# A Trainium2 decoder kernel's S5 stage: the output matrix made in compact form by VectorE and spread into blocks by ScalarE

## The reference, cut to what matters

```python
ab_re, ab_im, bb_re, bb_im = s5_discretize(lam_re, lam_im, log_dt, b_re, b_im)
bu_re = jnp.einsum("btgc,gpc->btgp", u, bb_re)
...
_, _, s_re, s_im = lax.associative_scan(_s5_combine, (a_re, a_im, bu_re, bu_im), axis=1)
y = (jnp.einsum("btgp,gcp->btgc", s_re, c_re.astype(jnp.float32))
     - jnp.einsum("btgp,gcp->btgc", s_im, c_im.astype(jnp.float32)))
```

## Time and profile before

| what | value |
|---|---|
| median of 3 runs | 3703.88 us (3703.57 to 3706.3) |
| the profiled execution, its own time | 3705.97 us |
| its span in the profile | 3704.4 us |
| TensorE matmul busy | 2222.4 us (60%) |
| VectorE busy | 2701.0 us (73%) |
| ScalarE busy | 590.1 us (16%) |
| GpSimd busy | 1227.0 us (33%) |
| S5 stage (to the first GLU product) | the first 232.5 us |

### The profile page before, as it was taken

How to read it: one execution, slowest core, us unless ns; L and a number is a source line. 1 busy time by engine, 2 the same in 40 slices (tenths; PEclk the granted TensorE clock), 3 DMA queues, 4 the chain that set the end, 5 groups by cost and what they waited for, 6 DMA issues and landing times.

```text
span 3704.4 us, 30645 instructions
## 1 busy us (share of the span) xinstructions
PE 2222.4 (60%) x9874; PEld 1420.6 (38%) x9874; DVE 2701.0 (73%) x3594; ACT 590.1 (16%) x1349; POOL 1227.0 (33%) x1366
## 2 busy tenths in 40 slices
PE   5789960002777786594997676440598771004776
PEld 5777750001222276593662366430254220001222
DVE  9931399998875588977578667869758559997554
ACT  6621100000111122200111112100111110000111
POOL 2110133433344332223333422224433444334332
PEclk9999985556999997797999988775799995557999
DMA  4023489999999999999999999999999999999998
GB/s 125 24 98 125 152 359 391 424 427 427 426 416 427 427 425 426 416 426 427 427 421 387 427 425 426 426 426 427 427 426 407 425 427 427 427 427 427 427 427 357
DMA packets 201715, 1407.16 MB, mean 380 GB/s; under 512 B 21856, under 2 KB 30304, under 8 KB 30768
## 3 DMA queue, kind: packets, MB, share of 16 engines
q0 software_dynamic: 167008, 1215.18, 78.1%
q1 hardware_dynamic: 34288, 190.10, 12.9%
q10 hardware_dynamic: 288, 0.18, 0.0%
HBM read 1402.13 MB, written 3.24 MB: 379 GB/s over the span
## 4 chain that ended last, share of the span: by engine, by line
DMA 40%; DVE 27%; PE 23%; issue 5%; ACT 4%; POOL 0%; DVEq 0%; POOLq 0%; ACTq 0%
DMA arena<-in_u_dram,ixs 27%; PE ps L937 15%; DVE arena L1782 14%; DMA arena<-in_v_dram,ixs 13%; PE ps L623 3%; ACT arena L1313 2%; DVE ps L1798 2%; PE ps L835 2%; PE ps L666 1%; DVE arena L1673 1%; DVE arena L1666 1%; DVE arena L1557 1%; DVE arena L1667 1%; DVE arena L1670 1%; DVE arena L1663 1%
## 5 line engine op out<-in xcount | busy, mean ns | idle before, releaser
L937 PE MATMUL ps<-arena 128*128 128x512 f32 x2304 | 1119.2, 616 | 1145.0 <-ACT arena L1313 1093.3
L1782 DVE CUSTOM_DVE_ANT_0 arena<-arena,ps 128x2048 f32<-128x2048 f32 x546 | 1234.1, 2286 | 195.7 <-DMA arena<-in_u_dram,ixs 177.3
L1798 DVE SCALAR_TENSOR_TENSOR ps<-arena,ps 128x1024 f32<-128x1024 f32 x564 | 727.0, 1289 | 532.2 <-DMA arena<-in_v_dram,ixs 513.0
L937 PEld LDWEIGHTS ps<-arena 128*128 128x128 f32 x2304 | 405.5, 192 | 1831.0 <-issue 953.3
L510 POOL DMA_INDIRECT arena<-in_u_dram,ixs x560 | 553.2, 988 | 1091.1 <-DVE arena L1782 1026.8
L510 POOL DMA_INDIRECT arena<-in_v_dram,ixs x576 | 558.7, 970 | 935.5 <-PE ps L937 634.2
L835 PE MATMUL ps<-HT,W 128*128 128x160 f32 (+1 forms) x3072 | 406.8, 294 | 73.5 <-ACT arena L1263 30.7
L835 PEld LDWEIGHTS ps<-HT,W 128*128 128x128 f32 x3072 | 401.3, 197 | 93.2 <-issue 76.8
L1313 ACT ACTIVATE arena<-ident,arena 128x128 f32<-128x128 f32 x576 | 228.4, 400 | 1005.7 <-PE ps L937 973.9
L863 PE MATMUL ps<-W,arena 128*128 128x128 f32 x1024 | 124.9, 283 | 41.2 <-DVE arena L1904 14.9
L863 PEld LDWEIGHTS ps<-W,arena 128*128 128x128 f32 x1024 | 121.1, 198 | 43.7 <-DVE arena L1904 15.1
(11 more groups left out here) (291 smaller groups left out, 1764.5 us busy)
## 6 DMA issues: line engine op xcount, KB each, us to landing
W<-in_slabs_dram SPq DMA_DIRECT2D x168, 1024.0 KB, 9.9
arena<-in_u_dram,ixs POOLq DMA_INDIRECT x576, 16.5
arena<-in_v_dram,ixs POOLq DMA_INDIRECT x576, 16.7
HN<-in_s_bc_dram SPq DMA_DIRECT2D x16, 256.0 KB, 3.3
GB<-in_norms_dram POOLq DMA_DIRECT2D x4, 1024.0 KB, 12.1
X<-in_x_dram SPq DMA_DIRECT2D x3, 1024.0 KB, 13.7
W<-in_x_dram SPq DMA_DIRECT2D x8, 256.0 KB
out_y_dram<-HN SPq DMA_DIRECT2D x2, 1024.0 KB, 6.8
```

Of the source, the lines that this page charges most:

```text
L937: mm = nc.tensor.matmul(ps[:, 8 - SHARE + b, :], DG[(first + n) % DIAGS], ring[:, r, OWN + BANK * b:OWN + BANK * (b + 1)], start=(n == 0), ...
L1782: V.tensor_tensor_reduce(ring[:, r, :], ring[:, r, :], token, 1.0, 0.0, ALU.mult, ALU.add, AV[:, COL_AT[t] + n:COL_AT[t] + n + 1]).then_in ...
L1798: V.scalar_tensor_tensor(to, row, weight, total, ALU.mult, ALU.add).then_inc(row_used[r], 1)
```

## The change

`output_matrices(n)` no longer writes the four blocks of `OMX`. VectorE waits (`s5_ca`) until ScalarE has read the last compact matrix, and subtracts at full width, 128x512, twice, into two new buffers `CS`. ScalarE has a new step `output_blocks(n)`, between `chunk_columns(n+1)` and `kernels(n)`: it waits for `s5_cs` and `s5_y`, copies `CS` into the blocks of `OMX` by four copies of 64x512, and raises `s5_ca`, which so far VectorE raised. `input_matrices` keeps its four half-width subtractions, written out in place. `CS` lies in space that nothing else uses during the stage. No transfer is added or moved.

```diff
--- before.py
+++ after.py
@@ -228,6 +228,7 @@
         SP = [view(2 * D + 2 * PQ * CHUNKS * h, 2 * PQ * CHUNKS, w_flat).rearrange("p (c q j) -> p c q j", c=2, q=PQ)
               for h in range(2)]
         DEC = [view(2 * D + 4 * PQ * CHUNKS + 512 * h, 512, w_flat).rearrange("p (q j) -> p q j", q=PQ) for h in range(2)]
+        CS = [view(16384, 512), view(7424, 512, w_flat)]
         S0 = GB[:, 1, 0:1024].rearrange("p (c q b) -> p c q b", c=2, q=S5_Q)
         SSO = GB[:, 1, 1024:2048].rearrange("p (c q b) -> p c q b", c=2, q=S5_Q)
         U4 = ht_flat.rearrange("p (q j) -> p q j", q=S5_Q)
@@ -313,7 +314,7 @@
         s5_bc_in = [sem("s5_bc_in0"), sem("s5_bc_in1")]
         s5_bcc, s5_dd, s5_h, s5_ends = sem("s5_bcc"), sem("s5_dd"), sem("s5_h"), sem("s5_ends")
         s5_ph, s5_f, s5_tab, s5_dec = sem("s5_ph"), sem("s5_f"), sem("s5_tab"), sem("s5_dec")
-        s5_ab, s5_ca, s5_pad = sem("s5_ab"), sem("s5_ca"), sem("s5_pad")
+        s5_ab, s5_cs, s5_ca, s5_pad = sem("s5_ab"), sem("s5_cs"), sem("s5_ca"), sem("s5_pad")
         s5_k, s5_kc = sem("s5_k"), sem("s5_kc")
         s5_bs, s5_c0, s5_g = sem("s5_bs"), sem("s5_c0"), sem("s5_g")
         s5_tp, s5_tc = sem("s5_tp"), sem("s5_tc")
@@ -1097,6 +1098,18 @@
                             scale=(1.0, -1.0)[c])
                 ins.then_inc(s5_c0, 1)
 
+            def output_blocks(n):
+
+                act.wait_ge(s5_cs, n + 1)
+                if n > 0:
+                    act.wait_ge(s5_y, n)
+                for c in range(2):
+                    for h in range(2):
+                        rows = slice(64 * h, 64 * (h + 1))
+                        ins = A(OMX[rows, c, :, 1:, 16 * h:16 * (h + 1)], CS[c][rows].rearrange("p (q s n) -> p q s n", q=PQ, s=LC),
+                                ACT.Copy)
+                ins.then_inc(s5_ca, 1)
+
             def kernels(n):
 
                 act.wait_ge(s5_k, n + 1)
@@ -1150,6 +1163,7 @@
                 if more:
                     turned_inputs(n + 1)
                     chunk_columns(n + 1)
+                output_blocks(n)
                 kernels(n)
                 if n > 0:
                     token_rows(n - 1)
@@ -1540,7 +1554,7 @@
                 V.scalar_tensor_tensor(PRD, plus, ROUND, PRD, ALU.subtract, ALU.subtract).then_inc(s5_f, 1)
                 dve.wait_ge(s5_f, n + 1)
 
-            def scaled(to, n, first, tables, free):
+            def scaled(n, first, tables):
 
                 qs, cube4 = slice(PQ * n, PQ * (n + 1)), [P, PQ, LC, 16]
                 re, im, neg = (w[:, :, qs].rearrange("p s q -> p q s").unsqueeze(3).to_broadcast(cube4) for w in tables)
@@ -1550,34 +1564,33 @@
                 V.tensor_tensor(t[1], b, im, ALU.mult)
                 V.tensor_tensor(t[2], a, neg, ALU.mult)
                 settle(V.tensor_tensor(t[3], b, re, ALU.mult))
-                free()
+                return t
+
+            def input_matrices(n):
+
+                dve.wait_ge(s5_bcc, n + 1)
+                t = scaled(n, 0, (GFR, GFI, GFN))
+                if n > 0:
+                    dve.wait_ge(s5_tp, S5_TURN[INPUT, n - 1, 3] + 1)
+                    dve.wait_ge(s5_bs, n)
                 for c in range(2):
                     for h in range(2):
                         rows = slice(64 * h, 64 * (h + 1))
-                        ins = V.tensor_tensor(to[rows, c, :, :, 16 * h:16 * (h + 1)], t[2 * c][rows], t[2 * c + 1][rows],
+                        ins = V.tensor_tensor(IMX[rows, c, :, :, 16 * h:16 * (h + 1)], t[2 * c][rows], t[2 * c + 1][rows],
                                               ALU.subtract)
-                return ins
-
-            def input_matrices(n):
-
-                def free():
-                    if n > 0:
-                        dve.wait_ge(s5_tp, S5_TURN[INPUT, n - 1, 3] + 1)
-                        dve.wait_ge(s5_bs, n)
+                ins.then_inc(s5_ab, 1)
+                dve.wait_ge(s5_ab, n + 1)
+
+            def output_matrices(n):
 
                 dve.wait_ge(s5_bcc, n + 1)
-                scaled(IMX, n, 0, (GFR, GFI, GFN), free).then_inc(s5_ab, 1)
-                dve.wait_ge(s5_ab, n + 1)
-
-            def output_matrices(n):
-
-                def free():
-                    if n > 0:
-                        dve.wait_ge(s5_y, n)
-
-                dve.wait_ge(s5_bcc, n + 1)
-                scaled(OMX[:, :, :, 1:], n, 2, (PWR, PWI, PWN), free).then_inc(s5_ca, 1)
-                dve.wait_ge(s5_ca, n + 1)
+                scaled(n, 2, (PWR, PWI, PWN))
+                if n > 0:
+                    dve.wait_ge(s5_ca, n)
+                for c in range(2):
+                    ins = V.tensor_tensor(CS[c], T[2 * c], T[2 * c + 1], ALU.subtract)
+                ins.then_inc(s5_cs, 1)
+                dve.wait_ge(s5_cs, n + 1)
 
             def states(n):
```

## The result

The changed kernel takes **3731.13 us** (median of 6 runs, 3727.30 to 3732.37), the kernel before in the same session 3704.08 (3703.55 to 3708.13): a ratio of 1.0068, 95% interval [1.0057, 1.0080], or +27 us. Slower, as forecast; but the forecast was 3716.7, and the range ended at 3729.0. The rival that came true is the first one, with the clock much worse (3722 to 3733).

A forecast was written before the change was run, and what follows sets the result against it. The loop through ScalarE's compaction and TensorE's kernel was taken as the bound, not VectorE's occupancy. Place-by-place terms of +7.4 us plus +5.4 for the clock gave +12.8 on 3703.88: 3716.7 us, range 3706.5 to 3729.

The forecast's parts named there:

- the first one, with the clock much worse: Rival: transposes and kernels at the low clock in most pairs, +18 to +29 us, 3722 to 3733; chance 0.17.
- the clock's price for the transposes: TensorE's input transposes, slower behind a longer pause: 0.4 us a pair, over six pairs.
- The bound: S5 loop of compaction, matrices, TensorE's kernel, ScalarE's copies, 23.68 us; VectorE, nearly full, waits once a pair for the compaction.
- The copies and the route: Four ScalarE copies ahead of the kernel take 2.49 us; ScalarE's route becomes 13.11 us against 11.76, +1.35 a pair.
- kernel term: TensorE's kernel product, slower by the clock behind a longer pause: 0.5 us a pair.
- the predicted loop: One middle pair of the S5 stage by the route alone: 25.03 us for 23.68.
- the mechanism and the bound: Sixteen transposes wholly at the low clock take 2.2 us more; ScalarE's copies hide all but 1.4.
- outputs 0 and kernel 7: TensorE restarts used to size the clock term: 2.46 us idle then 5.13 low; 3.15 idle then 5.46, no more than now.
- The pause itself: TensorE's pause behind the outputs, ahead of the input transposes: to grow from 1.29 to 2.3 us.
- The outputs' wait for the states: TensorE's outputs no longer wait 0.96 us for the states, so the pause behind them grows.
- GpSimd's collision: GpSimd's phases may hold up an input matrix instead of the output matrix; ScalarE's route hides it, otherwise 0.7 us a pair.
- the sum of +12.8: Whole forecast loss: +7.4 us from the places in the S5 stage and +5.4 from the clock.

The follow-up runs named there:

- e4: Changed kernel with its two full-width subtractions cut into four of 64 rows each; 3728.46 us, ratio 1.0062.
- e1: Changed kernel plus 16 extra TensorE transposes of a constant ahead of each pair's input transposes and 16 ahead of its kernel product; 3703.01 us, ratio 0.9993.
- e10: Changed kernel plus 16 extra TensorE transposes ahead of each pair's input transposes alone; 3721.23 us, ratio 1.0041.
- e15: Changed kernel with GpSimd's phase held back until VectorE's input subtractions are done; 3728.26 us, ratio 1.0063.
- e12: Changed kernel with the second half of each pair's outputs held back on TensorE until VectorE's third product of the next input matrix; 3719.78 us, ratio 1.0041.
- e6: Changed kernel with ScalarE's compaction of the next input moved ahead of its kernels copy; 3709.03 us, ratio 1.0012.
- e3: Kernel before plus the change's four ScalarE copies at the same queue place, into spare buffers nobody waits for; 3704.67 us, ratio 0.9996.
- e14: e6 with TensorE's kernel product begun on the output matrix's real part, the imaginary part afterwards, all sums complete; 3698.23 us, ratio 0.9980.

## Why the prediction was wrong

The term that failed is the clock's price for the transposes, 0.4 us a pair: the stretch that holds them grew by 1.87.

- **The bound, right.** The loop led through the compaction, not through VectorE's 22.9 busy microseconds. e4 undoes VectorE's gain at no cost that can be measured.
- **The copies and the route, right.** Four copies of 2.52 us (2.49 predicted). From the last chunk copy to the next kernel's copies +1.80 us, where route and kernel term, 1.35 + 0.5, gave 1.85; the kernel took 5.98 us for some 5.4 before. With the clock held up, e1 has 23.73 us a pair; the predicted loop of 25.03, with e1's kernel of 3.88 us in place of 5.4, is 23.5.
- **Where it failed: "0.4 for the transposes".** The first stretch grew by 1.87 us instead. e10 gives 1.55 of it to the clock. The rest, some 0.3, is in e1 too: there the last chunk copy ends 17.1 us after the kernel's copies, with a collision but no clock loss. Of it 0.23 lies ahead of the compaction, which starts 5.37 us after the kernel's copies for 5.14 before. The prediction had the mechanism and the bound (two times 1.09 us more, of which ScalarE hides all but 1.4; e10's 1.55 lies even above that) and then chose a value near the favourable end, by outputs 0 and kernel 7, which say nothing of short products that ScalarE takes away one by one. Kernel 7 was misread as well: it did not begin at the low clock, as its first four products took 0.60 us, like those of kernel 6, which ran at the full clock. It fell to the low one on its way. In the middle pair the kernel already ran its first half low and had little left to lose; the transposes, with 1.09 us for eight at the full clock behind a pause of 1.29 us, had everything.
- **The pause itself was underestimated,** 2.3 us foretold and 3.42 measured. The outputs' wait for the states was added to it, as foretold; the collision (0.75) and a compaction that ends some 0.2 later were not. By e15 this did not decide: behind 2.67 us the clock was low as well.
- **GpSimd's collision, right:** the input subtractions took the 0.75 us, and ScalarE's route hid most of it (0.07 us on the kernel's start in e10 against e12, 0.28 us a pair in e15).
- **Place by place.** Kernel 0 started at 52.87 (53.03 foretold), the GELU behind it at 67.62 (67.7). Kernel 1 came at 78.41, not at 75.5: the same transposes, 3.90 us long behind a pause of 2.79. Kernel 1 to 6 took 135.6 us, not 129.65; kernel 6 to 7 was 0.4 us shorter than before, as foretold; from kernel 7 to the stage's end, 1.4 us less was foretold and 0.4 more came, as the kernel ran 6.5 us for 5.5 and outputs 7 8.2 us for 7.5. So of the 14.2 us by which +27.0 exceeds the sum of +12.8, some 2.9 came ahead of kernel 1, 6.0 between kernels 1 and 6, and 1.8 behind kernel 7; the other 3.6 lie outside the stage or between profile and median, for which the sum has no term.
- **The chances.** Direction and mechanism held, and the outcome lay among the cases named, under "the clock gets much worse" (0.17). What spoke against it there, kernel 7, was one restart of another product, and misread.

The Trainium skill, page "TensorE: Matmul & The Clock Gate", section "HAM oscillation — how this bites in real kernels", describes a loop in which the wait of every pass lets the clock fall, so that each piece of work starts slow. The traces agree, pair by pair (0.50 in the transposes, 0.63 in the kernel, 1.00 in e1).

Not settled: what exactly decides. The second eight transposes of e6 ran at the full clock in the pair shown (1.11 us) and at the low one in the pair before it (1.94 us), behind the same pause of 2.67 us. Kernel 7 of e3 ran its 3.91 us at a clock of 1.00 behind 3.15 us, the pause behind which kernel 7 of the kernel before had 0.69; kernel 6 of e3 had 0.66 behind 0.42 us. So the length of the one pause ahead of a product does not by itself foretell its clock. Kernel 7 of e3:

```profile
210.40 0.60 PE L737 MATMUL ps<-arena 128*32 128x128 f32 x4 [3.15 <-DVE arena L1562]
```

## What to carry to other kernels

When work moves from a nearly full engine to an idle one, ask who waits for it there: the copies cost nothing on a queue that nobody follows (e3) and a loop's length where TensorE stands behind them. Then list TensorE's pauses before and after, and take into the range the low clock for every product behind a longer pause, those that ran at the full clock first of all. A pause can be cut by order (compaction early, a product begun on its first half, outputs split); that brought the clock back for most of the transposes (e12, e6) but not for the kernel (e14). And even useless transposes paid here, as they held the clock up.

## What was not expected of the hardware

- An added wait, with no other work, took some 10 us from the program (ratios of 1.0041 and 1.0068; what it moved of GpSimd is worth 0.28 us a pair by e15). It cut one stretch of idle time in two, and the transposes behind it ran at 1.00 instead of 0.50.
- Extra TensorE work of nearly 4 us a pair shortened the pair by 3.6 us (e1).
- VectorE's half-width subtractions ran 3.54 us for 2.79 beside GpSimd's phase of 1.5 us. The collision follows the phase: with the phase moved they take 2.79 us (e15), and before the change a product beside it took 1.42 us for 0.69.
